# Moving the axpys of a value-reduction loop ahead of a weight split on VectorE

## The reference

```python
a = jnp.einsum('td,thkd->thk', hb, u[ib])            # dot with the chosen rows of peer_u
coef = wb * jax.nn.gelu(a, approximate=False)
out = jnp.einsum('thk,thkd->td', coef, v[ib])        # weighted sum of the chosen rows of peer_v
x = _layer_norm(DEEPNORM_ALPHA * x + g2 * out, ln2_g, ln2_b)
```

## Time and profile before

| | |
|---|---|
| median of 3 runs | 4735.66 us (4731.47 to 4737.82) |
| the profiled execution, its own time | 4731.47 us |
| its span in the profile | 4729.7 us |
| mean granted TensorE clock | 0.955 of full speed |
| down loop, first to last matmul | about 3591 to 4709 us of the span |

### The profile page before, as it was taken

The page is one execution under the profiler, slowest core; times in us unless marked ns, Lnnn a source line. Parts: engine busy times, 40 slices in busy tenths (PEclk is TensorE's granted clock), DMA queues, the critical chain, the costliest instruction groups (busy, mean ns, idle before and its releaser), DMA issues.

```text
span 4729.7 us, 58551 instructions
## 1 busy us (share of the span) xinstructions
PE 4304.7 (91%) x21163; PEld 3649.8 (77%) x21163; DVE 2986.7 (63%) x3412; ACT 1386.6 (29%) x1485; POOL 1252.6 (26%) x643
## 2 busy tenths in 40 slices
PE   7799999999988998779899999699997899999997
PEld 2588777777766876668899999698896687788886
DVE  0334665445544653455699999476775677788887
ACT  0322332333332121132233454122222233333332
POOL 0001333000001320023465544476773111112220
PEclk9899999999999998879899999799998899999999
DMA  8325666000003665257455577999997899999995
GB/s 290 98 74 155 185 183 180 34 31 16 31 33 97 189 191 108 71 141 162 111 147 139 131 176 181 310 359 355 359 353 265 332 342 339 342 343 380 381 375 190
DMA packets 716549, 967.22 MB, mean 204 GB/s; under 512 B 137467, under 2 KB 535859, under 8 KB 680371
## 3 DMA queue, kind: packets, MB, share of 16 engines
q1 hardware_dynamic: 638531, 613.29, 42.7%
q0 software_dynamic: 40928, 285.23, 15.8%
q10 hardware_dynamic: 37008, 67.65, 4.9%
HBM read 896.84 MB, written 69.22 MB: 204 GB/s over the span
## 4 chain that ended last, share of the span: by engine, by line
PE 55%; DMA 17%; DVE 14%; issue 7%; ACT 4%; SPq 1%; POOL 1%; DVEq 1%; ACTq 0%; POOLq 0%
PE ps L115 17%; PE ps L116 16%; PE ps L117 16%; DMA pu<-in_peer_u_dram 8%; DMA gel<-gelu_scratch 6%; DVE oneJ L1716 3%; DVE pT L1623 2%; DMA wm<-in_w_mod_dram 2%; PE ps L1881 1%; DVE mred L1314 1%; DVE vDl L1434 1%; DVE ring L1738 1%; PE ps L2039 1%; ACT wh L804 1%; DVE oneI L1717 1%
## 5 line engine op out<-in xcount | busy, mean ns | idle before, releaser
L115 PE MATMUL ps<-h2h,pTuh 128*128 128x384 f32 x2048 | 709.1, 346 | 94.0 <-POOL pTul L728 93.0
L728 POOL TENSOR_TENSOR pTul<-pT,pTuh 128x1024 fp32r<-128x1024 f32 x256 | 650.4, 2542 | 510.4 <-ACT pTuh L1082 509.0
L117 PE MATMUL ps<-h2h,pTul 128*128 128x384 f32 x2048 | 696.9, 340 | 0.0
L116 PE MATMUL ps<-h2l,pTuh 128*128 128x384 f32 x2048 | 696.6, 340 | 0.0
L115 PE MATMUL ps<-vDh,coh 128*128 128x512 f32 x1536 | 606.5, 395 | 53.0 <-DVE col L1434 52.4
L116 PE MATMUL ps<-vDl,coh 128*128 128x512 f32 x1536 | 602.2, 392 | 0.0
L117 PE MATMUL ps<-vDh,col 128*128 128x512 f32 x1536 | 601.8, 392 | 0.0
L704 POOL TENSOR_TENSOR mbuf<-mbuf,silu 128x2048 f32<-128x2048 f32 x64 | 255.8, 3996 | 1002.8 <-DMA mbuf<-in_w_mod_dram 1002.1
L1082 ACT ACTIVATE pTuh<-pT 128x1024 fp32r<-128x1024 f32 x256 | 271.8, 1062 | 847.5 <-DVE pT L1623 843.7
L115 PEld LDWEIGHTS ps<-h2h,pTuh 128*128 128x128 f32 x2048 | 394.2, 192 | 103.7 <-POOL pTul L728 87.4
L1623 DVE STREAM_TRANSPOSE pT<-pu 128x1024 f32<-128x1024 f32 x256 | 317.3, 1240 | 223.3 <-DMA pu<-in_peer_u_dram 170.7
(11 more groups left out here) (328 smaller groups left out, 8025.4 us busy)
## 6 DMA issues: line engine op xcount, KB each, us to landing
vraw<-in_peer_v_dram SPq DMA_DIRECT2D x128, 1024.0 KB, 8.7
mbuf<-in_w_mod_dram SPq DMA_DIRECT2D x64, 1024.0 KB, 6.1
pu<-in_peer_u_dram ACTq DMA_DIRECT2D x256, 256.0 KB
pu<-in_peer_u_dram SPq DMA_DIRECT2D x256, 256.0 KB
wraw<-in_w_in_dram SPq DMA_DIRECT2D x48, 1024.0 KB, 8.5
wt<-route_scratch SPq DMA_DIRECT2D x128, 384.0 KB, 7.2
gel<-gelu_scratch SPq DMA_DIRECT2D x128, 384.0 KB, 11.9
wm<-in_w_mod_dram SPq DMA_DIRECT2D x16, 2048.0 KB, 8.7
```

The costliest lines, as they stand in the source:

```text
L115: pe.matmul(out, lh, rh, start=first, stop=False)
L116: pe.matmul(out, lh, rl, start=False, stop=False)
L117: return pe.matmul(out, ll, rh, start=False, stop=last)
L728: pool.tensor_tensor(pTul[s][:, c, :], pT[s][:, c, :], pTuh[s][:, c, :].bitcast(fp32), ALU.subtract).then_inc(u_lo, 1)
```

## The change

In the loop over the pairs the axpys of pair n move up: from behind `down_coef_lo(n)` to right behind `down_coef(n)`, and so ahead of `down_v_lo(n)`, of `gate_diag` and of `down_coef_lo(n)`. No instruction is added or taken away, and all waits stay with their instructions.

```diff
             for n in range(2, NK):
                 down_coef(n)
+                for k in range(ax_before(n), ax_before(n + 1)):
+                    axpy(k)
                 down_v_lo(n)
                 if 2 <= n < 6:
                     gate_diag(n - 2)
                 down_coef_lo(n)
-                for k in range(ax_before(n), ax_before(n + 1)):
-                    axpy(k)
                 if n == PAIRS:
```

## The result

After the change the kernel takes 4795.74 us (median of 4 runs, 4784.73 to 4804.99), beside 4736.57 us before in the same comparison: a ratio of 1.0126, interval 1.0103 to 1.0149. The forecast was 4741 us, its range ended at 4775. The profiled execution took 4789.41 us, its span is 4787.7 us.

A forecast was written before the change was run, and what follows sets the result against it. Transfers were taken to pace the first stretch of the down loop, TensorE the second. 3.1 + 2 = 5 us on the profiled 4731.5 gave 4736.5, or 4741 us against the runs' median, range 4731 to 4775.

The forecast's parts named there:

- What bounds the kernel.: Down loop: transfers pace 3811 to 4175 us; TensorE paces 4187 to 4640 us, transfers close behind.
- the 9 us of the first stretch: From 3811 to 4175 us, TensorE's pairs take 0.21 us above their floor, some 9 us in all.
- The 2.35 us are then paid once, not in each pair: Path from `gel` landing to TensorE's start: with landings unmoved, later pairs shift equally and the loop ends 3.1 us later.
- Can it shrink? ... I take 0 for the pairs with one axpy.: Flight of later-issued `gel` loads: 9.4 us needed, at most 8.0 seen, so 0 us for pairs with one axpy.
- by as much: Sign of being right: the median `vraw` flight falls like that of `gel`, by about 2.3 us.
- as long as the queue never runs dry: Condition on the load queue under which a `gel` load issued 2.35 us later lands at the same time.
- The pairs with two axpys: 11 pairs from 70 to 120: loop another 2.35 us longer, 2 us taken in all, at most 11 us.
- The gathers ... so nothing.: Gathers issued 3.2 us earlier after a landing; none is waited for in either stretch, so 0 us.
- the queue runs dry: Rival: late `vraw` leaves DMA engines idle about each landing; 4770 us at 0.3 us per pair; chance 0.40.
- the flight of at most 8.0 us: Pair 18's `gel` load, issued when the queue had just run empty; the evidence put against the queue running dry.

The follow-up runs named there:

- e8: Kernel before the change, with `vDl` made ahead of the multiplication: 4743.77 us, ratio 1.0018.
- e13: Kernel before, with third buffers for `vraw`, `gel` and `wt` from pair 18 and the `ln2_g`, `ln2_b` loads moved to the loop's end: 4719.09 us, ratio 0.9963.
- e14: The changed order of VectorE, with third buffers for `vraw`, `gel` and `wt` from pair 18 and `ln2_g`, `ln2_b` loaded late: 4727.00 us, ratio 0.9969.
- the small gathers: Kernel after the change, gathers of slots 66 to 127 cut to an eighth of their bytes: 4741.81 us; control, the same cut before the change: 4737.68 us.
- e7: Kernel before, only the `gel` load of pair n+2 held until VectorE ended the axpys of pair n: 4732.70 us, ratio 0.9996.
- e12: The change made in pairs 2 to 63 only, later pairs keeping the old order: 4743.33 us, ratio 1.0007.
- e4: Kernel after the change, with each gather held until `col` of its pair is made: 4800.71 us, ratio 1.0132.
- e1: Kernel after the change, but axpys moved only in pairs with one axpy; pairs with two keep both behind `col`: 4778.32 us, ratio 1.0086.
- e2: Kernel after the change, but axpys moved only in the 11 pairs with two axpys: 4761.77 us, ratio 1.0047.

## Why the prediction was wrong

- **What bounds the kernel.** Held: the first stretch paced by transfers, the second at TensorE's floor with the transfers close behind. e8, e13 and e14 show that the 9 us of the first stretch can be had.
- **"The 2.35 us are then paid once, not in each pair", 3.1 us.** Right for the path itself: 6.4 us from landing to TensorE in pair 42, and the small gathers, which leave this path alone, come out 4 us above their control. That agrees with it, but the intervals overlap: it is too small to be measured.
- **"Can it shrink? ... I take 0 for the pairs with one axpy."** The step that failed. I worked with the flight of `gel` alone and checked whether it could fall from 12.3 to 9.4 us. It can (8.8 us from 4187 to 4640 in e7), and it is free. The set is headed by `vraw`, whose flight I expected to fall "by as much"; it stayed at 9.3 us (e12), and its late start opens a gap in the queue: "as long as the queue never runs dry" was the condition, and it didn't hold. For pairs 2 to 63 the 0 came out right (e12), but by luck, as far as the reason goes: it hangs on the gather's new place (e4 against the change), which I had put at nothing. From pair 66 on, where the load on the DMA engines is higher, moving the pairs with one axpy costs 37 us (e1) where I had 0.
- **"The pairs with two axpys", 2 us, at most 11.** The same error: they cost 20 us alone (e2), 1.9 us each instead of 0.2.
- **"The gathers ... so nothing."** In sum about right (e4 and the change take the same time), but by the counts made up of some 21 us won in one stretch and 10 us lost in the other.
- **The rival "the queue runs dry"** named place and mechanism, and had 0.40. I priced it at 0.3 us per pair with 4770, spread over 98 pairs. Measured, nearly all of it lies in the 55 pairs from 66 to 120, 1.1 us for each. Against it I put "the flight of at most 8.0 us" from pair 18: a bound for one load right behind the stall for `xfin`, not for a loop at a DMA share of 0.98. The same place shows what an empty queue costs: with `vraw` issued at 3773.60 the DMA engines moved 116 GB/s from 3774 to 3776 us. And I left out what follows a stop of TensorE: a third of the loss (19.7 of 55.5 us) is slower matmuls, mostly the clock behind the stops, not the stops.

Open stays, beside the gather's part, how the 60 us divide between the two kinds of pairs when they act together. Alone they cost 37 and 20 us, but in stretch B alone e1 has 44 us (195 matmuls) and e2 28 us (124), together more than the change's 55.5. That 44 is more than 37 shows again what one execution is worth. The cycle in which two pairs run together was read from the trace and not taken apart.

## What to carry to other kernels

Where two buffers are reloaded on release, ask of every reordering when the next set of loads is issued and what the DMA engines do until then; here, at a DMA share of 0.98, a delay of the first load by one to three microseconds in each pair cost 18 to 104 us in all, at 0.95 it hung on what else was queued, and the last load of the set could be 1.9 us late for nothing. Test it by holding one load at a time and by cutting the bytes, and if room can be found, try a third set of buffers: it made the consumer's order all one here. Price a stop of TensorE with the slow stretch behind it.

## What the runs showed of the hardware that was not expected

Behind a stop of 4.1 us TensorE was granted 0.50 of its clock, and in the 8 us from 4248 it did 23 matmuls where 35 would be normal. Over 4187 to 4640 us of the change, at a mean of 0.95, slower matmuls made 19.7 us.

A gather's bytes come late behind its issue: in pair 42 the issue ended at 3989.51 us and its queue moved 0.01 MB until 3992, then 1.05 MB until 3998.

GpSimd's gather took longer to issue while VectorE worked on two tiles in SBUF. Groups of GpSimd, 3811 to 4175 us, after the change:

```profile
L742 POOL DMA_INDIRECT ring<-in_peer_v_dram,sidx x42 | 116.2, 2767 | 244.1 <-DVE acc L1761 244.1
```

It was 0.94 us before, in VectorE's pause. With the change each gather begins just as `vDl` does (3986.76 and 3986.41 in pair 42) and takes 2.75 us. In e14 the issue is back at 0.94 us (40.29 us for 43), and there VectorE waits for `vDh` at that moment: a gather at 4002.63, `vDl` at 4004.23. The kernel before has both cases too: from 3811 us on all 57 gathers whose issue falls in a pause of VectorE took 0.94 or 0.95 us, and the 12 that begin beside an axpy 3.0 in the median. GpSimd had nothing else to do; whether the longer issue delays the gather's bytes was not taken apart.
